# Splitting the last row, the bias copies and the first weight chunk differently at the edge between two fused blocks

## The reference

```python
x = layer_norm(alpha * x + conv_ffn(x, ...), ln_ffn_g[1], ln_ffn_b[1])   # end of block one, layer 1
...
h = rms_norm(x, norm_g) * (1.0 + scale) + shift                          # start of block two
proj = h @ w_in                                                          # 512 x 1024 by 1024 x 4224
...                                                                      # bias = rel_bias[:, rel_idx] in the attention
```

## Time and profile before

| | us |
|---|---|
| median of 3 runs (1783.92 to 1784.6) | 1784.28 |
| the profiled execution's own time | 1786.04 |
| its span, first to last instruction | 1784.2 |
| PE busy in the span | 1758.9 (99%) |
| DVE busy | 1027.2 (58%) |
| ACT busy | 652.2 (37%) |
| POOL busy | 99.5 (6%) |

### The profile page before, as it was taken

How to read it: one execution, slowest core, us unless ns; L and a number is a source line. 1 busy time by engine, 2 the same in 40 slices (tenths; PEclk the granted TensorE clock), 3 DMA queues, 4 the chain that set the end, 5 groups by cost and what they waited for, 6 DMA issues and landing times.

```text
span 1784.2 us, 27491 instructions
## 1 busy us (share of the span) xinstructions
PE 1758.9 (99%) x11571; PEld 1472.9 (83%) x11571; DVE 1027.2 (58%) x1480; ACT 652.2 (37%) x1013; POOL 99.5 (6%) x136
## 2 busy tenths in 40 slices
PE   8999999999999999999999999999999999999998
PEld 7888988988888889888998888888888767777766
DVE  5567267444445555454726755566556585566784
ACT  5232352323324333213235232232343553344552
POOL 3102002000000001000200200000001000011000
PEclk9999999999999999999999999999999999999999
DMA  9323312433333324333331264444431422112512
GB/s 302 111 94 113 113 49 77 147 95 102 98 95 107 94 83 128 109 95 117 108 107 60 89 195 153 142 154 130 138 94 36 151 60 73 38 38 63 176 36 83
DMA packets 146010, 189.67 MB, mean 106 GB/s; under 512 B 7800, under 2 KB 95092, under 8 KB 145120
## 3 DMA queue, kind: packets, MB, share of 16 engines
q1 hardware_dynamic: 140928, 172.59, 31.2%
q0 software_dynamic: 3488, 10.07, 1.8%
q10 hardware_dynamic: 1472, 5.26, 0.8%
HBM read 181.58 MB, written 6.30 MB: 105 GB/s over the span
## 4 chain that ended last, share of the span: by engine, by line
PE 93%; DVE 4%; issue 1%; ACT 1%; POOL 1%; DMA 0%; SPq 0%; DVEq 0%; ACTq 0%
PE ps L329 28%; PE ps L331 27%; PE ps L330 27%; PE ps L970 2%; PE ps L518 1%; PE ps L2222 1%; PE ps L2242 1%; PE ps L1628 1%; PE ps L2236 1%; PE ps L2256 0%; DVE LATE L2303 0%; PE ps L2359 0%; PE ps L982 0%; DVE WL L313 0%; PE ps L1652 0%
## 5 line engine op out<-in xcount | busy, mean ns | idle before, releaser
L313 DVE TENSOR_TENSOR WL<-RAW,WH 128x1024 fp32r<-128x1024 f32 x289 | 350.8, 1223 | 501.3 <-ACT WH L303 500.0
L329 PE MATMUL ps<-XH,WH 128*128 128x512 f32 (+1 forms) x1416 | 524.6, 371 | 3.4 <-DVE XL L1498 1.6
L303 ACT ACTIVATE WH<-RAW 128x1024 fp32r<-128x1024 f32 x289 | 303.5, 1058 | 597.5 <-PE ps L331 570.0
L331 PE MATMUL ps<-XH,WL 128*128 128x512 f32 (+1 forms) x1416 | 518.2, 366 | 0.0
L330 PE MATMUL ps<-XL,WH 128*128 128x512 f32 (+1 forms) x1416 | 517.9, 366 | 0.0
L329 PE MATMUL ps<-WH,XH 128*128 128x512 f32 x784 | 312.7, 399 | 2.4 <-DVE WL L313 1.1
L329 PEld LDWEIGHTS ps<-XH,WH 128*128 128x128 f32 x1416 | 267.5, 189 | 51.4 <-issue 6.1
L331 PE MATMUL ps<-WH,XL 128*128 128x512 f32 x784 | 305.8, 390 | 0.0
L330 PE MATMUL ps<-WL,XH 128*128 128x512 f32 x784 | 305.5, 390 | 0.0
L331 PEld LDWEIGHTS ps<-XH,WL 128*128 128x128 f32 x1416 | 267.4, 189 | 43.4
L330 PEld LDWEIGHTS ps<-XL,WH 128*128 128x128 f32 x1416 | 267.7, 189 | 40.9
(11 more groups left out here) (359 smaller groups left out, 1797.5 us busy)
## 6 DMA issues: line engine op xcount, KB each, us to landing
RAW<-ffn_w_up SPq DMA_DIRECT2D x176, 256.0 KB, 3.2
RAW<-ffn_w_down SPq DMA_DIRECT2D x44, 512.0 KB, 3.7
RAW<-w_in SPq DMA_DIRECT2D x33, 512.0 KB, 3.9
RAW<-xa_wkv SPq DMA_DIRECT2D x32, 512.0 KB, 3.8
RAW<-c_w_in SPq DMA_DIRECT2D x24, 512.0 KB, 3.8
LATE<-w_ada SPq DMA_DIRECT2D x24, 512.0 KB, 4.8
RAW<-xa_wq SPq DMA_DIRECT2D x16, 512.0 KB, 5.7
RAW<-xa_wo SPq DMA_DIRECT2D x16, 512.0 KB, 3.7
```

The source lines that it names most:

```text
L303: e.activation(halves_of(i)[0][:, :, 0:w], raw(i)[:, :, 0:w], ACT.Copy).then_inc(*w_hi.up(i))
L313: e.tensor_tensor(wl[:, :, 0:w], raw(i)[:, :, 0:w], wh[:, :, 0:w].bitcast(F), ALU.subtract).then_inc(*w_lo.up(i))
L329: e.matmul(o, lh, rh, start=start, stop=False)
L331: return e.matmul(o, ll, rh, start=False, stop=stop)
```

## The change

Six edits, all in the passage.

1. The place of a weight half becomes `(i + 4) % 5` for the first 248 chunks.
2. ACT calls `hi_to(248 + 1)` and DVE calls `lo_to(248 + 1)` before they start on row 0. Chunks 249 and 250 are made by ACT later, between the `XH` tiles; DVE keeps its own two at k = 2 and 4.
3. Bias tiles 0, 2 and 3 are copied by ACT, tile 1 by DVE inside row 3.
4. Row 3's last scale and add, and its square, are done in halves of 512; POOL folds the first half's sum in; `xn` of row 3 is made by ACT for 256 channels and by DVE for the other 768.
5. The transposes go rows 0 to 2 for k = 0 to 3, rows 0 to 2 for k = 4 to 7, then row 3 for all k.
6. `XH` of k = 0 is written by ACT straight from PSUM, `gemm_t` waits for `XH` and `XL` apart in its first chunk and takes the products with `XL` last, and ACT's order of tiles changes.

```diff
-    half_of = [i % NH for i in range(n_in2)] + ...
+    half_of = [(i + 4) % NH for i in range(n_in2)] + ...
@@ gemm_t
+            if ready and c == 0:
+                for kt in range(2):
+                    e.wait_ge(*ready(x_hi, kt))
+                    for m in range(nm):
...
+                        e.matmul(bs[m][:, 0:ntok], wh[:, kt, ms], XH[:, kt, 0:ntok], start=kt == 0, stop=False)
+                        e.matmul(bs[m][:, 0:ntok], wl[:, kt, ms], XH[:, kt, 0:ntok], start=False, stop=False)
+                    e.wait_ge(*ready(x_lo, kt))
+                    for m in range(nm):
...
+                r.then_inc(*gemm.up(("used", i)))
+                continue
@@ down_act, l == 1
+            hi_to(e, n_in2 + 1)
             for t in range(2):
                 square_act(e, t)
                 xn_act(e, t)
             square_act(e, 2)
-            hi_to(e, n_in2 + 1)
+            bias_act(e, 0)
             xn_act(e, 2)
-            bias_act(e, 0)
-            bias_act(e, 1)
-            hi_to(e, n_in2 + 2)
-            square_act(e, 3)
-        hi_to(e, min(first[(*n, 1)] + 11 + NH, n_in2 + 3))
-        if l == 1:
-            xn_act(e, 3)
+            bias_act(e, 2)
+            bias_act(e, 3)
+            for half in range(2):
+                square_last_act(e, half)
+            xn_last_act(e)
@@ down_dve, l == 1
+        lo_to(e, n_in2 + 1)
         for t in range(4):
             ln_in_dve(e, (*n, 1), 1, t)
+            if t == 3:
+                last_row_dve(e, n)
+                continue
...
-        bias_dve(e, 2)
-        bias_dve(e, 3)
-        e.wait_ge(*rms_g.at(3))
-        lo_to(e, min(first[(*n, 1)] + 11 + NH, n_in2 + 1))
+        xn_last_dve(e)
+    def last_row_dve(e, n):
...
+        bias_dve(e, 1)
...
+        for half in range(2):
+            cs = slice(512 * half, 512 * half + 512)
+            e.scalar_tensor_tensor(out=x[:, cs], in0=x[:, cs], scalar=rs[:, 3:4], in1=b[:, cs], op0=ALU.mult,
+                                   op1=ALU.add).then_inc(*ln_v.up((n, 3, half), (n, 3)))
+    def square_last_act(e, half):
...
+        e.activation(SCR[:, cs], XR[:, 3, cs], ACT.Square, accum_out=ss[:, 3:4] if half else sqa).then_inc(
+    def xn_last_act(e):
...
+        e.activation(xn[:, 3, 0:256], XR[:, 3, 0:256], ACT.Copy, scale=rq[:, 3:4]).then_inc(*rms_a.up(("xn", 3)))
+    def xn_last_dve(e):
...
+        e.tensor_scalar(xn[:, 3, 256:1024], XR[:, 3, 256:1024], rq[:, 3:4], None, ALU.mult).then_inc(*rms_v.up(("xn", 3)))
@@ h_rows_pe
+        for ks, ts in ((range(4), range(3)), (range(4, 8), range(3)), (range(8), (3,))):
@@ h_rows_act
+            if k == 0:
+                e.wait_ge(*h_pe.at(0))
+                e.activation(XH[:, 0, :], ps.tile(("h", 0))[:, :], ACT.Identity, scale=s1[:, 0:1],
+                             bias=mod[:, 0:1]).then_inc(*x_hi.up(("h2", 0)))
+                affine(1)
+                continue
+            if k == 2:
+                affine(3)
+            if k in (5, 7):
+                affine(k)
...
+            if k in (1, 3):
+                hi_to(e, n_in2 + 2 + k // 2)
```

More of the change, by code:

```diff
@@ L256, in programs @@
     raw_of = [i % NR for i in range(n_in2)] + [i % 3 for i in range(n_chunks - n_in2)]
-    half_of = [i % NH for i in range(n_in2)] + [i % 3 for i in range(n_out2 - n_in2)] + [0, 1, 2, 0, 1, 3, 4, 2]
+    half_of = [(i + 4) % NH for i in range(n_in2)] + [i % 3 for i in range(n_out2 - n_in2)] + [0, 1, 2, 0, 1, 3, 4, 2]
     def before(places, i):
@@ L343, in gemm_t @@
             e.wait_ge(*w_lo.at(i))
+            if ready and c == 0:
+                for kt in range(2):
+                    e.wait_ge(*ready(x_hi, kt))
+                    for m in range(nm):
+                        ms = slice(128 * m, 128 * m + 128)
+                        if kt == 0:
+                            for w in ps.vacant((stage, m)):
+                                e.wait_ge(*w)
+                        e.matmul(bs[m][:, 0:ntok], wh[:, kt, ms], XH[:, kt, 0:ntok], start=kt == 0, stop=False)
+                        e.matmul(bs[m][:, 0:ntok], wl[:, kt, ms], XH[:, kt, 0:ntok], start=False, stop=False)
+                    e.wait_ge(*ready(x_lo, kt))
+                    for m in range(nm):
+                        r = e.matmul(bs[m][:, 0:ntok], wh[:, kt, 128 * m:128 * m + 128], XL[:, kt, 0:ntok], start=False,
+                                     stop=False)
+                r.then_inc(*gemm.up(("used", i)))
+                continue
             for m in range(nm):
@@ L350, in gemm_t @@
                     if ready and m == 0:
-                        e.wait_ge(*ready(kt))
+                        e.wait_ge(*ready(x_lo, kt))
                     ms = slice(128 * m, 128 * m + 128)
@@ L1387, in down_dve @@
                                        op0=ALU.add, op1=ALU.mult).then_inc(*rms_v.up("s1"))
-        bias_dve(e, 2)
-        bias_dve(e, 3)
-        e.wait_ge(*rms_g.at(3))
-        lo_to(e, min(first[(*n, 1)] + 11 + NH, n_in2 + 1))
+        xn_last_dve(e)
+    def last_row_dve(e, n):
+        x, g, b = XR[:, 3, :], GB[:, 0:1024], GB[:, 1024:2048]
+        e.wait_ge(*latest["V"])
+        e.bn_aggr(mv[:, 3, :], stats[:, 3, 0:2, :]).then_inc(*ln_v.up((n, 3, "aggr")))
+        bias_dve(e, 1)
+        e.wait_ge(*ln_v.at((n, 3, "aggr")))
+        e.scalar_tensor_tensor(out=x, in0=x, scalar=mv[:, 3, 0:1], in1=g, op0=ALU.subtract,
+                               op1=ALU.mult).then_inc(*ln_v.up((n, 3, "g")))
+        e.wait_ge(*ln_v.at((n, 3, "g")))
+        e.wait_ge(*ln_g.at((n, 3)))
+        for half in range(2):
+            cs = slice(512 * half, 512 * half + 512)
+            e.scalar_tensor_tensor(out=x[:, cs], in0=x[:, cs], scalar=rs[:, 3:4], in1=b[:, cs], op0=ALU.mult,
+                                   op1=ALU.add).then_inc(*ln_v.up((n, 3, half), (n, 3)))
     s1, ss, rq = SM[:, 172:180], SM[:, 180:184], SM[:, 184:188]
@@ L1405, in xn_act, with rms_last_pool @@
         e.activation(xn[:, t, :], XR[:, t, :], ACT.Copy, scale=rq[:, t:t + 1]).then_inc(*rms_a.up(("xn", t)))
+    sqa = SM[:, 252:253]
+    def square_last_act(e, half):
+        cs = slice(512 * half, 512 * half + 512)
+        e.wait_ge(*ln_v.at((("ffn", 1), 3, half)))
+        e.wait_ge(*latest["A"] if half else rms_a.at(("sq", 2)))
+        e.activation(SCR[:, cs], XR[:, 3, cs], ACT.Square, accum_out=ss[:, 3:4] if half else sqa).then_inc(
+            *rms_a.up(("sq", 3, half)))
+    def xn_last_act(e):
+        e.wait_ge(*rms_g.at(3))
+        e.activation(xn[:, 3, 0:256], XR[:, 3, 0:256], ACT.Copy, scale=rq[:, 3:4]).then_inc(*rms_a.up(("xn", 3)))
+    def xn_last_dve(e):
+        e.wait_ge(*rms_g.at(3))
+        e.tensor_scalar(xn[:, 3, 256:1024], XR[:, 3, 256:1024], rq[:, 3:4], None, ALU.mult).then_inc(*rms_v.up(("xn", 3)))
+    def rms_last_pool(e):
+        e.wait_ge(*rms_a.at(("sq", 3, 0)))
+        e.tensor_scalar(sqa, sqa, 1.0 / D, 1e-6, ALU.mult, ALU.add).then_inc(*rms_g.up("ms half"))
+        e.wait_ge(*rms_g.at("ms half"))
+        e.wait_ge(*rms_a.at(("sq", 3, 1)))
+        e.tensor_scalar(ss[:, 3:4], ss[:, 3:4], 1.0 / D, sqa, ALU.mult, ALU.add).then_inc(*rms_g.up(("ms", 3)))
+        e.wait_ge(*rms_g.at(("ms", 3)))
+        e.tensor_tensor(rq[:, 3:4], ss[:, 3:4], nhalf[:, 0:1], ALU.pow).then_inc(*rms_g.up(3))
     def rms_pool(e, t):
@@ L1457, in h_rows_pe @@
             ps.take(("h", k))
[L1458 to L1466, removed]
+        for ks, ts in ((range(4), range(3)), (range(4, 8), range(3)), (range(8), (3,))):
+            for t in ts:
+                e.wait_ge(*rms_a.at(("xn", t)))
+                for k in ks:
+                    if t == 0:
+                        for w in ps.vacant(("h", k)):
+                            e.wait_ge(*w)
+                    if (t, k) == (3, 2):
+                        e.wait_ge(*rms_v.at(("xn", 3)))
+                    r = e.transpose(ps.tile(("h", k))[:, 128 * t:128 * t + 128], xn[:, t, 128 * k:128 * k + 128], ident)
+                    if t == 3:
+                        r.then_inc(*h_pe.up(k))
         ps.back(*[("h", k) for k in range(8)])
@@ L1481, in h_rows_act, with affine @@
         e.wait_ge(*rms_v.at("s1"))
-        for k in range(8):
[L1483 to L1493, removed]
+        def affine(k):
+            e.wait_ge(*h_pe.at(k))
+            if k >= 4:
+                e.wait_ge(*x_lo.at(("h2", k - 4)))
+            e.activation(hs[k % 4], ps.tile(("h", k))[:, :], ACT.Identity, scale=s1[:, k:k + 1],
+                         bias=mod[:, k:k + 1]).then_inc(*ps.empties(("h", k), h_a, k))
+        for k in range(8):
+            if k == 0:
[8 more added lines that the diff above has]
+                affine(k)
+            e.wait_ge(*(h_a if k % 2 else h_v).at(k))
+            e.activation(XH[:, k, :], hs[k % 4], ACT.Copy).then_inc(*x_hi.up(("h2", k)))
+            if k in (1, 3):
+                hi_to(e, n_in2 + 2 + k // 2)
     def h_rows_dve(e):
@@ L1497, in low @@
             e.wait_ge(*x_hi.at(("h2", k)))
+            if k == 0:
```

(11 more changed lines are left out.)

## The result

The changed kernel takes 1800.2 us (median of 4, 1798.63 to 1801.6) against 1784.13 (median of 4, 1783.92 to 1784.6). The ratio is 1.0089, interval 1.0072 to 1.0107: slower by 0.7 to 1.1%, in the forecast range of 1795.8 to 1801.5. Its profiled execution took 1799.19 us, span 1797.4.

A forecast was written before the change was run, and what follows sets the result against it. PE was taken as the bound, busy 1758.9 of 1784.2 us. Waits ahead of row 0 +17.26, rest of the edit -4.3, clock +1.1 gave +14.1 onto the median 1784.28: 1798.4 us, range 1795.8 to 1801.5.

The forecast's parts named there:

- The release by chunk 246: Ahead of row 0, ACT and DVE wait for this chunk's use to free chunk 248's place; row 0 moves by 17.26 us.
- The rows: Rows 0 to 3 follow each other at 5.43 us a step through ACT and POOL, whatever PE does.
- a spacing other than 5.4: Sign of being wrong: rows following each other faster or slower than 5.4 us.
- the bias copy: ACT's three and DVE's one, between POOL's steps of rows 2 and 3: 0.65 us each, said to cost nothing.
- From row 3's scale to the 96th product: Rest of the edit, to the projection's 96th product: 27.95 us at full clock against 32.25 before, 4.3 saved.
- The clock: 1.2 GHz level over most of 1387 to 1410, slowing five of the projection's products: +1.1 us, bounds 0 to +2.7.
- The sum: Whole passage: 17.26 - 4.3 + 1.1 = +14.1 us, put onto the median of 1784.28 for 1798.4.
- A clock that stays low for two more stretches: Rival at the projection: 6.6 us more at half clock, 15 products at +0.2, 1801.4 us; chance 0.08.
- The wait that does not stand there: Rival: chunk 248's place is free before row 0, all of the 17.26 is gone, 1780.5 us; chance 0.04.
- Absorption later: Rival: behind the passage, loads and recurrence run further ahead of PE, absorbing at most 2 to 3 us: 1795.5; chance 0.06.

The follow-up runs named there:

- The shifts of the place: Changed kernel with the place of a weight half as (i + 2), (i + 1), i or (i + 3) % 5: 1781.99, 1796.68, 1797.24, 1801.19 us.
- the waits alone: Kernel before the change with only (i + 4) % 5 for the places and chunk 248's two halves called for ahead of row 0: 1802.37 us, ratio 1.0096.
- holder 243: Changed kernel with (i + 2) % 5, so chunk 248's place was last held by chunk 243: 1781.99 us, ratio 0.9987.
- chunk 244: Changed kernel with (i + 1) % 5, so this chunk last held chunk 248's place: 1796.68 us, ratio 1.007.

## Why the prediction was right, point by point

**The release by chunk 246.** Right. ACT's line 303 began 1.11 us before PE's first bias product, forecast 1379.67 - 1378.56 = 1.11. Row 0 lay 16.13 us ahead of that product and is now 1.13 behind it: moved by 17.26, the number forecast. The shifts of the place and the waits alone confirm the cause. The Trainium skill, page "TensorE: Matmul & The Clock Gate", section "Architectural detail: the array is 16× 32×32, not 1× 128×128", states that ScalarE's and VectorE's queues are strictly first in, first out. The two idle times of 19 us agree with it: nothing that stood behind the two waits ran ahead of them.

**The rows.** Forecast 5.43 us apart; measured 5.10, 5.01 and 5.43. This is the step that I had read as fixed, "whatever PE does", and that is not; a spacing other than 5.4 was one of my own signs of being wrong. POOL's operation of line 685 (701 now) took 1.21 in the earlier trace rows because DVE's line 674 ran beside it, and it ended with it; and DVE's own work on a row had first waited for PE, 0.25 to 0.34 us at line 693 in the trace of before. When PE no longer paces the rows, DVE starts its operation earlier against POOL's, and less of it is left to wait for. POOL's timeline, changed kernel, rows 1 and 2:

```profile
1387.40 0.87 POOL L701 TENSOR_SCALAR SM<-SM 128x1 f32<-128x1 f32 x1
...
1392.50 0.80 POOL L701 TENSOR_SCALAR SM<-SM 128x1 f32<-128x1 f32 x1
```

1387.40 + 0.87 = 1388.27 and DVE's line 690 ends at 1386.91 + 1.28 = 1388.19. In row 3 the bias copy, which I had costed at nothing, stands ahead of that DVE operation, and the full 5.43 is back: it costs 0.4 here. In the kernel with the waits alone, which has no copy there, row 3's step is 1399.78 - 1394.77 = 5.01. Over three rows -0.76 us.

**From row 3's scale to the 96th product.** Forecast 27.95 at full clock and 1.1 for the clock, 29.05; measured 1429.14 - 1399.48 = 29.66. The terms that were mis-sized are short ones of row 3. The timelines of ACT and POOL, changed kernel:

```profile
1401.08 0.63 ACT L1444 ACTIVATE SCR<-XR 128x512 f32<-128x512 f32 x1
1401.62 0.19 ACT L1444 ACTIVATION_READ_ACCUMULATOR SCR<-XR 128x1 f32 x1
1402.91 0.51 ACT L1449 ACTIVATE BIG<-XR,SM 128x256 f32<-128x256 f32 x1 [1.11 <-POOL SM L1462]
```

```profile
1401.98 0.27 POOL L1460 TENSOR_SCALAR SM<-SM 128x1 f32<-128x1 f32 x1 [0.71 <-ACT SCR L1444]
1402.33 0.55 POOL L1462 TENSOR_TENSOR SM<-SM 128x1 f32<-128x1 f32 x1
```

Call the start of row 3's first half H, as the prediction does (1399.48). The second square with the read-out of its sum ends at H + 2.33 (1401.81), forecast 2.08; POOL's two end at H + 3.40, forecast 2.98; `xn` of 256 columns takes 0.51, forecast 0.4. The first transpose came at H + 4.00, forecast 3.5. Saved against the 32.25 of before: 2.6, not 3.2.

**The clock.** The low level held from 1386.0 to 1402.8 and came back for the first products (0.50 from 1406.4 to 1409.7). In between it was granted in full for one stretch in which PE had little to do (busy 1.62 of 3.30 us); the forecast had it low over most of 1387 to 1410 and did not have this stretch. It came behind a stretch in which the transposes, at half clock, kept PE busy for 3.33 of 3.80 us:

```profile
1399.00:1402.80 3.80, 3.33 (x16) 2.93 (x14) 1.41 (x2) 2.02 (x6) 1.30 (x4) 0.50 0.00 0
```

So the order seen in the earlier trace rows is seen here too: full clock behind the 3.33 of 3.80 us, half clock behind the 1.62 of 3.30. From T (1403.91, when ACT starts on the first tile of h) to the 96th product it was 25.2 us, forecast 25.0.

**The sum.** 17.26 - 0.76 - 2.59 = 13.9 in the traces, forecast 14.1. That it fits so closely is in part luck: the rows took 0.8 us less than forecast and the rest saved 0.6 us less, and the two errors nearly cancel. Between the medians it is 16.1. The 2.2 us between are not a further mechanism that the runs show: the profiled execution of before was 1786.04, 1.9 above its median, that of the change 1799.19, 1.0 below its own, and 1.9 + 1.0 + 13.15 (1799.19 - 1786.04) = 16.05 (the 13.15 are the 13.9 less the 0.7 that lie ahead of the passage). I had both the 1786.04 and the 1784.28 before me and set a difference worked out in the one onto the other; the two low stretches of the earlier trace rows are likely not both in most executions of the kernel before: its mean clock was 0.998 in the profiled one and in 24 of the 65 that ran beside the experiments, 0.999 or 1.000 in the other 41. The executions of the change differ likewise: mean clock 0.992 and 0.993 at 1801.6 and 1801.2, 0.994 in the other two.

**The rivals.** A clock that stays low for two more stretches: not in this trace. The wait that does not stand there: made to happen with holder 243, 1781.99 where 1780.5 was worked out. Its condition, release before 1361, was met (1358.75); with chunk 244, released at 1374.8, all but 3.5 us of the loss is there, as the condition says. Absorption later: none seen.

## What to carry to other kernels

Before a piece of work is moved ahead in an engine's list, work out which earlier use must end before its buffer comes free; a place in a rotation is part of the schedule, and here one number in it was worth 18 us. A wait named at one engine can be caused by the order of another engine's list (DVE, POOL, ACT here), so follow it to the instruction that stands ahead. Set the trace that a sum is made in against the median of its runs before adding the one to the other. And where differences of 1 or 2 us count, read the clock of every execution first: here much of what the smaller edits seemed worth went with it.

## What the runs showed of the hardware

A POOL operation on one column of SBUF takes 0.22 us alone, and ends 0.08 to 0.09 us behind a DVE operation with two SBUF operands of 128 x 1024 that began ahead of it: it takes up to 1.31 us where the row order sets them side by side, 0.22 when DVE was made to wait, and 0.22 too in row 3 with holder 243, where DVE was copying from PSUM at the time (the timelines of POOL and DVE there):

```profile
1381.24 0.22 POOL L701 TENSOR_SCALAR SM<-SM 128x1 f32<-128x1 f32 x1
```

```profile
1381.11 0.69 DVE L1536 COPY VH<-ps 128x512 f32<-128x512 f32 x1
```

The Trainium skill, page "SBUF — State Buffer", section "Terms", states that DVE and GpSimd share a port pair that one of them holds for its full instruction while the other blocks; for POOL behind DVE these numbers agree. The other way round no row here shows it: in the changed kernel DVE's line 690 took its usual 1.28 us from 1386.91, though an operation of POOL (line 1468) had begun at 1386.77 and ran for 0.55. Holding DVE back freed POOL, yet the rows took 1.2 us longer: DVE's 1.28 then stands in the row's chain instead of beside POOL's.
